# The SSD mixer of a two-block transformer kernel, with pair loop, norms and transposes re-ordered and the decay built by float32r matmuls

## The reference, cut to what matters

```python
def ssd_mixer(u, w_in, conv_w, conv_b, dt_bias, a_log, d_skip, norm_w, w_out):
    proj = u @ w_in                     # z: 2048, xbc: 3072, dt: 32
    xbc = silu(causal_dwconv(xbc, conv_w, conv_b))   # x: 2048, B: 4*128, C: 4*128
    dt = softplus(dt_raw + dt_bias);  a = -exp(a_log)
    y = ssd_chunked_scan(xs, dt, a, bm, cm) + d_skip[:, None] * xs
    y = gated_group_rmsnorm(y, z, norm_w)            # y * silu(z), norm over 512 channels
    return y @ w_out

# ssd_chunked_scan: 4 chunks of 128 positions, 32 heads of 64 channels, 4 groups of 8 heads
cs = cumsum(dt * a)                                   # within a chunk, per head
decay_in = exp(where(tri, cs[l] - cs[s], -inf))
y_diag = ((C @ B.T) * decay_in) @ (x * dt)
states = B.T @ (x * dt * exp(cs[-1] - cs))            # per chunk
entering = sum over earlier chunks of states * decay between chunks
y_off = (C @ entering) * exp(cs)
```

## Time and profile before

| | |
|---|---|
| median of three runs (3233.7 to 3242.68) | 3242.62 us |
| the profiled execution: its own time | 3239.93 us |
| its span | 3237.8 us |
| mean granted TensorE clock | 0.948 |
| busy: PE, PEld | 3023.4 us (93%), 2446.9 us (76%) |
| busy: DVE, ACT, POOL | 1459.0, 1178.9, 1307.8 us |
| the SSD mixer | from the start to 556 us |

### The profile page before, as it was taken

One profiled execution on the slowest core, in us unless ns is written; L12 is line 12 of the kernel. 1 busy time (PEld: TensorE's weight loads), 2 busy tenths in 40 slices (PEclk: granted clock), 3 DMA queues, 4 the chain that ended last, 5 costly groups with the idle time before them and its releaser, 6 DMA issues.

```text
span 3237.8 us, 33761 instructions
## 1 busy us (share of the span) xinstructions
PE 3023.4 (93%) x13476; PEld 2446.9 (76%) x13476; DVE 1459.0 (45%) x2111; ACT 1178.9 (36%) x1640; POOL 1307.8 (40%) x670
## 2 busy tenths in 40 slices
PE   6989979999999878999999998899999989999998
PEld 4866647888888766788888877797888867778886
DVE  5557761651352377354155056663422345433132
ACT  4422233542343455543244253003423334343232
POOL 4411105544444436544444546103444443054443
PEclk8989989999999989999999998579999999999999
DMA  2211103222223222233333322002323221022322
GB/s 111 95 37 40 39 14 104 92 97 94 96 97 98 72 69 67 90 98 98 98 98 98 97 79 72 1 1 65 105 93 103 86 85 64 14 91 91 104 93 83
DMA packets 74172, 253.11 MB, mean 78 GB/s; under 512 B 8353, under 2 KB 8353, under 8 KB 74017
## 3 DMA queue, kind: packets, MB, share of 16 engines
q1 hardware_dynamic: 73008, 247.55, 23.8%
q10 hardware_dynamic: 1008, 3.41, 0.3%
HBM read 248.83 MB, written 2.10 MB: 77 GB/s over the span
## 4 chain that ended last, share of the span: by engine, by line
PE 84%; DVE 8%; ACT 3%; issue 2%; DMA 1%; POOL 1%; DVEq 0%; POOLq 0%; ACTq 0%; SPq 0%
PE bank L366 22%; PE bank L368 22%; PE bank L367 22%; PE bank L1495 3%; PE bank L388 2%; PE bank L389 1%; PE bank L390 1%; PE bank L440 1%; PE bank L843 1%; PE bank L845 1%; PE bank L844 1%; DVE inv L446 1%; PE bank L856 1%; DVE lth L1340 1%; POOL wlo L2189 1%
## 5 line engine op out<-in xcount | busy, mean ns | idle before, releaser
L2189 POOL TENSOR_TENSOR wlo<-raw,whi 128x1024 fp32r<-128x1024 f32 (+2 forms) x497 | 1135.8, 2288 | 1842.4 <-ACT whi L311 1842.4
L311 ACT ACTIVATE whi<-raw 128x1024 fp32r<-128x1024 f32 (+2 forms) x497 | 501.3, 1009 | 1139.6 <-DMA raw<-in_f_up 487.2
L366 PE MATMUL bank<-h_hi,whi 128*128 128x512 f32 x2240 | 878.8, 392 | 24.5 <-ACT xbc L925 17.2
L367 PE MATMUL bank<-h_lo,whi 128*128 128x512 f32 x2240 | 873.7, 390 | 0.0
L368 PE MATMUL bank<-h_hi,wlo 128*128 128x512 f32 x2240 | 873.4, 390 | 0.0
L366 PEld LDWEIGHTS bank<-h_hi,whi 128*128 128x128 f32 x2240 | 422.3, 189 | 116.6 <-ACT xbc L925 17.7
L367 PEld LDWEIGHTS bank<-h_lo,whi 128*128 128x128 f32 x2240 | 422.1, 188 | 89.9 <-issue 2.2
L368 PEld LDWEIGHTS bank<-h_hi,wlo 128*128 128x128 f32 x2240 | 422.0, 188 | 87.8
L366 PE MATMUL bank<-act_hi,whi 128*128 128x512 f32 x864 | 336.2, 389 | 0.9 <-POOL wlo L2189 0.9
L368 PE MATMUL bank<-act_hi,wlo 128*128 128x512 f32 x864 | 336.1, 389 | 0.0
L367 PE MATMUL bank<-act_lo,whi 128*128 128x512 f32 x864 | 336.1, 389 | 0.0
(11 more groups left out here) (418 smaller groups left out, 3886.0 us busy)
## 6 DMA issues: line engine op xcount, KB each, us to landing
raw<-in_f_up SPq DMA_DIRECT2D x216, 512.0 KB, 3.5
raw<-in_f_dn SPq DMA_DIRECT2D x64, 512.0 KB, 3.4
raw<-in_ssd_xbc SPq DMA_DIRECT2D x24, 512.0 KB, 3.5
raw<-in_f_dn SPq DMA_DIRECT2D x32, 384.0 KB, 3.0
raw<-in_lru_in SPq DMA_DIRECT2D x20, 512.0 KB, 3.5
raw<-in_ev_in SPq DMA_DIRECT2D x20, 512.0 KB, 3.5
raw<-in_f_dn SPq DMA_DIRECT2D x32, 320.0 KB, 2.9
raw<-in_ssd_z SPq DMA_DIRECT2D x16, 512.0 KB, 3.5
```

Of the source, the lines that this page charges most:

```text
L311: act.activation(whi[:, s, 0:WIDTH[u]], raw[:, s, 0:WIDTH[u]], ACT.Copy).then_inc(hi_done, 1)
L366: pe.matmul(out, wh, hi, start=kt == 0, stop=False)
L367: pe.matmul(out, wh, lo, start=False, stop=False)
L2189: pool.tensor_tensor(wlo[:, s, 0:n], raw[:, s, 0:n], whi[:, s, 0:n].bitcast(F32), ALU.subtract)\
```

## The change

The mixer's work is re-ordered and partly moved:

- The dt chain moves to xbc tile 8 on VectorE and ScalarE. It now covers 128 partitions, and ends with csT cut into three fp32r parts (`cs3`, rows 0 to 31, 32 to 63 and 64 to 95). The small transposes follow tile 13, and x's transposes follow tiles 15 to 22, two sets each; VectorE takes two sets behind each tile from 16 on.
- The decay of a head is built in its bank by six fp32r matmuls: `sel3` spreads the row over the partitions, `ident_r` with `mask_r` adds -2^100 above the diagonal, and four matmuls of 128 columns, one for each chunk, take the head's own sum off. ScalarE's exp is then taken in the bank without a bias, and VectorE multiplies by C.B from there. One more fp32r matmul with `selp` gives the rows for both heads of a pair, and one exp serves both (`ec`). GpSimd builds `selp` (`pair_rows`).
- The entering part of y is a product of its own in bank 2 for both heads, scaled by `ec` afterwards.
- The group norms move into the loop, one group behind: squares summed by GpSimd and TensorE, the inverse by Ln and Exp, the low half on GpSimd, which also makes `xdd` (`decayed`).
- z uses banks 0 and 1, the output product banks 4, 5, 0 and 1. Eight z blocks go with each pair.

```diff
+        ident_r = at("ident_r", place["ident_r"], [P, P], F32R)
+        sel3 = at("sel3", place["sel3"], [P, 64], F32R)
+        selp = at("selp", BIG + 87 * KB, [P, 2, P], F32R)
...
+            def x_natural(i):
                 st.freed(pe, i)
                 if i == 0:
-                    pe.wait_ge(nat_ok, 1)
-                    pe.wait_ge(et_ok, 1)
+                    pe.wait_ge(dt_dve, 7)
+                    pe.wait_ge(dt_act, 9)
                 w(pe, xdt_ok, i - 1)
                 for c in range(NC):
                     last = pe.transpose(bank[4 + i % 2][:, c * P:(c + 1) * P], xbc[:, i, c * P:(c + 1) * P], ident[:])
                 last.then_inc(tr_x, 1)
...
+            def decay_rows(i):
+                if i == 0:
+                    pe.wait_ge(xdt_ok, NX)
+                w(pe, p_S, 2 * i)
+                for e in range(2):
+                    h = 2 * i + e
+                    pe.matmul(bank[4 + e][:], sel3[0:96, h:h + 1].broadcast_to((96, P)), cs3[0:96, :], start=True, stop=False)
+                    pe.matmul(bank[4 + e][:].rearrange("p (c l) -> p c l", c=NC), ident_r[:],
+                              mask_r[:].unsqueeze(1).broadcast_to((P, NC, P)), start=False, stop=False)
+                    for c in range(NC):
+                        last = pe.matmul(chunk(bank[4 + e], c), chunk(cs3[0:96, :], c),
+                                         sel3[0:96, 32 + h:33 + h].broadcast_to((96, P)), start=False, stop=c == NC - 1)
+                    last.then_inc(p_cs, 1)
+                g, q = (i - 1) // 4, (i - 1) % 4
+                w(pe, p_ec, i)
+                if i == 0:
+                    pe.wait_ge(g_ent, 2)
+                elif q == 1:
+                    w(pe, gn_inv, g)
+                elif q == 2 and g + 1 < SSD_G:
+                    pe.wait_ge(g_bn, g + 2)
+                elif q == 3:
+                    pe.wait_ge(g_ent, 3 * g + 5)
+                pe.wait_ge(p_sel, i + 1)
+                pe.matmul(bank[6][:], selp[0:96, i % 2, :], cs3[0:96, :], start=True, stop=True).then_inc(p_c2, 1)
+            def y_entering(i):
+                g, q = i // 4, i % 4
+                pe.wait_ge(g_ent, 3 * g + 3)
+                pe.wait_ge(p_xd, i + 1)
+                for c in range(1, NC):
+                    last = pe.matmul(chunk(bank[2], c), ent[:, c - 1, q * P:q * P + P], chunk(xbc[:, 20 + g, :], c),
+                                     start=True, stop=True)
+                last.then_inc(p_off, 1)
+            def y_diagonal(i):
+                g, q = i // 4, i % 4
+                w(pe, p_ev, i)
+                for e in range(2):
+                    pe.wait_ge(p_S, 2 * i + e + 1)
+                    for c in range(NC):
+                        last = pe.matmul(bank[3][64 * e:64 * e + 64, c * P:(c + 1) * P],
+                                         xdt[:, g, c, q * P + 64 * e:q * P + 64 * e + 64], chunk(t1[:, e, :], c),
+                                         start=True, stop=True)
+                last.then_inc(p_y, 1)
...
+            def squares(g, ec_read):
+                pe.wait_ge(gn_acc, 2 * g + 2)
+                pe.wait_ge(p_ec, ec_read)
+                pe.matmul(bank[6][:], ones[:], nacc[:], start=True, stop=False)
+                pe.wait_ge(gn_sq, 4 * g + 4)
+                pe.matmul(bank[6][:], ones[:], sqg[:], start=False, stop=True).then_inc(gn_mm, 1)
+            for t in range(2, 24):
+                st.pe_tile(pe, t, rhs_h)
+                if t == 13:
+                    natural()
+                if 15 <= t <= 22:
+                    x_natural(2 * t - 30)
+                    x_natural(2 * t - 29)
+            c_b(0)
+            b_natural(0, 0)
+            z_blocks(2)
+            states(0, 0)
+            states(0, 1)
+            z_blocks(2)
+            decay_rows(0)
+            states(0, 2)
+            z_blocks(4)
+            for i in range(NX):
+                g, q = i // 4, i % 4
+                y_entering(i)
+                if q == 1 and g:
+                    squares(g - 1, i + 1)
+                if q == 2 and g + 1 < SSD_G:
+                    b_natural(g + 1, i + 1)
+                if q == 3 and g + 1 < SSD_G:
+                    states(g + 1, 0)
+                    states(g + 1, 1, i + 1)
+                z_blocks(4)
+                y_diagonal(i)
+                if i + 1 < NX:
+                    decay_rows(i + 1)
+                if q == 2 and g + 1 < SSD_G:
+                    c_b(g + 1)
+                if q == 3 and g + 1 < SSD_G:
+                    states(g + 1, 2)
+                z_blocks(4)
...
+                act.wait_ge(dt_dve, 3)
+                act.activation(dd[:, 1, :], dd[:, 1, :], ACT.Exp).then_inc(dt_act, 1)
+                act.activation(cs3[:], csT[:], ACT.Copy).then_inc(dt_act, 1)
+                act.wait_ge(dt_dve, 5)
+                act.activation(cs_mid[:], dd[:, 0, :], ACT.Copy).then_inc(dt_act, 1)
+                act.activation(cs3[32:64, :], dd[32:64, 0, :], ACT.Copy)
+                act.wait_ge(dt_dve, 6)
+                act.activation(cs3[64:96, :], dd[64:96, 2, :], ACT.Copy).then_inc(dt_act, 1)
...
+                if t == 8:
+                    dt_chain()
+                if t == 16:
+                    act.wait_ge(tr_dt, 2)
+                    act.activation(etot[:].rearrange("p a b -> p (a b)"), bank[5][:, 0:P], ACT.Exp).then_inc(dt_act, 1)
...
+            def exps(i):
+                act.wait_ge(p_c2, i + 1)
+                w(act, p_om, i)
+                act.activation(ec[:], bank[6][:], ACT.Exp).then_inc(p_ec, 1)
+                for e in range(2):
+                    h = 2 * i + e
+                    act.wait_ge(p_cs, h + 1)
+                    act.activation(bank[4 + e][:], bank[4 + e][:], ACT.Exp).then_inc(p_E, 1)
...
+            def inverse(g):
+                act.wait_ge(gn_mm, g + 1)
+                act.activation(bank[6][:], bank[6][:], ACT.Ln, bias=eps[:], scale=1.0 / 512).then_inc(gn_ln, 1)
+                act.wait_ge(gn_ln, g + 1)
+                act.wait_ge(g_ent, 3 * min(g + 2, SSD_G))
+                act.activation(bank[7][:], bank[6][:], ACT.Exp, scale=-0.5).then_inc(gn_inv, 1)
...
+            keep_b(0)
+            keep_cb(0)
+            exps(0)
+            for i in range(NX):
+                g, q = i // 4, i % 4
+                if i:
+                    z_tanh_of(i - 1)
+                if q == 1 and g:
+                    inverse(g - 1)
+                if q == 2 and g + 1 < SSD_G:
+                    keep_b(g + 1)
+                if q >= 2 and g:
+                    for k in (2 * q - 4, 2 * q - 3):
+                        high(4 * g - 4 + k)
+                if i + 1 < NX:
+                    exps(i + 1)
+                if q == 2 and g + 1 < SSD_G:
+                    keep_cb(g + 1)
+                if i:
+                    square(i - 1)
+            z_tanh_of(NX - 1)
+            square(NX - 1)
+            inverse(SSD_G - 1)
+            for k in range(4):
+                high(12 + k)
...
+                if 16 <= t:
+                    x_natural(2 * t - 32)
+                    x_natural(2 * t - 31)
...
+            def gate(i):
+                b = zt.bank(i)[:]
+                zt.tile_ready(dve, i)
+                dve.tensor_tensor(b, b, ipre[:], ALU.mult).then_inc(z_scaled, 1)
+                dve.wait_ge(z_tanh, i + 1)
+                dve.scalar_tensor_tensor(out=b, in0=zr[:], scalar=1.0, in1=b, op0=ALU.add, op1=ALU.mult).then_inc(z_gate, 1)
+                dve.wait_ge(z_gate, i + 1)
+                dve.wait_ge(p_ev, i + 1)
+                dve.scalar_tensor_tensor(out=xbc[:, i, :], in0=xbc[:, i, :], scalar=0.5, in1=b, op0=ALU.mult,
+                                         op1=ALU.mult).then_inc(zt.free(i), 1)
+                zt.freed(dve, i)
+                dve.engine_nop().then_inc(p_g, 1)
+            def y_sum(i):
+                dve.wait_ge(p_y, i + 1)
+                dve.tensor_tensor(xbc[:, i, :], bank[3][:], xbc[:, i, :], ALU.add).then_inc(p_ev, 1)
+            def normed(j):
+                dve.wait_ge(gn_inv, j // 4 + 1)
+                dve.scalar_tensor_tensor(out=xbc[:, j, :], in0=xbc[:, j, :], scalar=col("ssd_norm", j), in1=bank[7][:],
+                                         op0=ALU.mult, op1=ALU.mult).then_inc(gn_n, 1)
+            st.freed(dve, 22)
+            dve.memset(bank[2][:, 0:P], 0.0).then_inc(p_xd, 1)
+            entering(0)
+            y = bank[2][:, P:T]
+            for i in range(NX):
+                g, q = i // 4, i % 4
+                dve.wait_ge(p_off, i + 1)
+                dve.wait_ge(p_ec, i + 1)
+                dve.tensor_tensor(y, y, ec[:, P:T], ALU.mult).then_inc(p_om, 1)
+                dve.wait_ge(p_om, i + 1)
+                dve.scalar_tensor_tensor(out=xbc[:, i, :], in0=xbc[:, i, :], scalar=col("ssd_d", i), in1=bank[2][:],
+                                         op0=ALU.mult, op1=ALU.add).then_inc(p_xd, 1)
+                if i:
```

(98 more changed lines are left out.)

333 lines of the change are left out of this document (136 added, 197 removed).

## The result

The changed kernel takes 3307.16 us (median of 4, 3304.72 to 3309.6) against 3238.16 us (median of 4, 3233.41 to 3242.68) for the kernel before: ratio 1.0213, 95% interval [1.019, 1.0236]. It is slower by 69 us; I had forecast 11.4 us more, 3254, with a range to 3280. The profiled execution took 3304.78 us, with a span of 3302.9, 65.1 above the span before.

A forecast was written before the change was run, and what follows sets the result against it. TensorE, busy 93%, was taken as the bound. Convolution stage +43.6, loop +10.1 and norms -42.3 gave +11.4 us: 3239.9 to 3251.3 profiled, 3254 as median; own range 3240 to 3268, 8 in 10 from 3218 to 3280.

The forecast's parts named there:

- Conv stage: Convolution tiles up to C.B of group 0: C.B starts at 243.1 instead of 199.5, +43.6 us.
- xdt stops: Convolution tiles 16 to 22: TensorE stands 4.65 us behind each for VectorE's xdt, seven times.
- restart cost: Convolution tiles after a stop: the next tile's first matmuls run at the low clock, losing 1.5 us.
- Start of the loop: Mixer's pair loop, from C.B to t1 of pair 0 complete: 20.8 us with a cold restart.
- One pair: Mixer's pair loop: period 12.45 us; C.B to the last pair 231.8 against 221.7 us, +10.1.
- The relay: Pair loop: VectorE, ScalarE, GpSimd in turn delay selp; seventh matmul waits until A+5.15, A being t1 complete.
- signs of being wrong: Stated failure tests: short xdt waits, selp never releasing TensorE, or decay matmuls passing 5 us after t1.
- Rival (b): Pair loop: TensorE doesn't wait for GpSimd's rows; pair falls to 9.9, about 39 us less, 3215; chance 0.10.
- The clock: Pair loop: 8 us allowed for TensorE's clock falling; 0 if it never falls, 28 at worst.
- rival (c): Pair loop runs cold: 20 us more, 3277; chance 0.14 together with tiles that stay cold.
- The narrow matmul: Decay's 128-column fp32r matmuls: start spacing bounded by 0.09 and 0.225 us; the choice said not to matter.
- Norms: Last pair to end of first two output tiles: 26.5 us instead of 68.8, -42.3, with norms inside the loop.

The follow-up runs named there:

- e_xfix: Changed kernel with VectorE taking the transposed x sets one tile earlier and etot computed ahead of tile 15; 3253.36 us.
- e_gate: Changed kernel with VectorE's sum and gate of a pair right behind that pair's t1, and its tanh at the head of ScalarE's round; 3258.85 us.
- e_order: Changed kernel with x sets taken a tile earlier, sum and gate right behind t1, and the three holders of bank 6 brought forward; 3167.47 us.
- e_rows: Changed kernel with only GpSimd's order changed: pair_rows for the next pair ahead of the split of z's low parts; 3307.34 us.
- e_bias: Changed kernel without the four 128-column matmuls per head; ScalarE's exp takes the head's column as bias, chunk by chunk; 3290.51 us.

## Why the prediction was wrong

**Conv stage, +43.6.** Right: +41.0. The order of the code gave the xdt stops before the trace could (4.65 forecast from a row of the kernel before, seven times 4.65 measured). The restart cost is right too: behind the set at 190.80 the tile's first eight matmuls take 3.55 us (192.39 to 195.94) where eight warm ones take 1.8, so 1.7 lost where I took 1.5. e_xfix takes that whole term away: the delay was the order of two loops, not work. By the rule that I weighed there (the Trainium skill, "TensorE: Matmul & The Clock Gate", Part 4: transposes don't bring full clock) a tile would have lost up to 2.9. The rows lie nearer to my value, but they can't say what the transposes did for the rise: it came at 195.9, after 3.5 us of fp32r matmuls.

**Start of the loop, 20.8.** Right: t1 of pair 0 was complete 20.7 us after `C.B`.

**One pair, +10.1 for the loop. This is the step that failed**, and it carries the error: from `C.B` to the end of the last pair 293.2 us, not 231.8, so +71.5 and not +10.1. The step says that the seventh matmul waits for `selp` and that "four z blocks 2.74" lie behind it to cover VectorE's 3.2. I priced those z blocks and never asked what they wait for. The two z banks are named in the change; with them the first z block of a tile can't start before `gate(i-1)`, and that is behind t1(i). So VectorE's chain isn't covered by z: it is followed by scaling, tanh and gate (309.15 to 311.9; TensorE stands 4.2 us there, in the fourteen stops 5.1 on average), then by the z blocks, the first eight of their twelve matmuls at 1.2 GHz (0.43 a start in place of 0.23), and only then by `y_diagonal`. t1 to t1 took 270.1 us in the fifteen intervals (18.0 each) against 210.1 with the clock's 8. The miss in these intervals is 60 us. e_gate shows the cause of most of it: with the gate (and the sum and tanh that it needs) moved ahead, the wait is gone and 49 us of the loop with it, though new stops of 31.4 us came at L917. With those away too (e_order) the loop is 82 us shorter than in the kernel after, and shorter than I had forecast. What the cut to two z banks has in it by itself is read from the code; no run gives z a third bank.

**The relay.** Its time was right: `selp` was complete at 314.55, 5.3 us behind t1, where I had put the seventh matmul at A+5.15. What was wrong is that TensorE waits for it: it comes to L917 only at 319.88, 10.7 behind t1, and e_rows gives nothing. Two of my signs of being wrong thus came true: `selp` never releases TensorE, and the decay matmuls pass A+5. Rival (b) had that, but expected a faster kernel from it: a wait that doesn't bind gives nothing back when another is longer. **The clock.** I put down 8 us. In the shares above, 25 us lie between the loop with and without its stops. So rival (c)'s effect was there, but with the stops at the z blocks and not with a stop at the decay. **The narrow matmul.** My lower bound was right (0.10 us), but "it doesn't matter" was not: as the relay doesn't bind, it lies on TensorE's path, 17 us in e_bias.

**Norms, -42.3.** Right: from the last `y_diagonal` (533.7) to the end of the first output tiles (557.65) 24.0 us. The same mark in the kernel before lies at 489.55, not at my rounded 490, so the stage took 68.4 there and the change is -44.4. The rows in the kernel after:

```profile
540.43 1.28 ACT L1069 ACT_TABLE_LOAD   x1
...
545.58 1.02 PE L947 MATMUL bank<-sqg,ones 128*128 128x512 f32 x2
546.64 0.66 ACT L1069 ACTIVATE bank<-bank,eps 128x512 f32<-128x512 f32 x1 [4.93 <-PE bank L947]
547.32 1.28 ACT L1072 ACT_TABLE_LOAD   x1
548.62 0.58 ACT L1072 ACTIVATE bank<-bank 128x512 f32<-128x512 f32 x1
...
550.72 5.03 POOL L2381 TENSOR_TENSOR g_lo<-xbc,g_hi 128x512 fp32r<-128x512 f32 x4 [8.68 <-ACT g_hi L1076]
551.71 0.39 PE L398 MATMUL bank<-g_hi,wlo 128*128 128x512 f32 x1
552.08 0.50 PE L396 MATMUL bank<-g_hi,whi 128*128 128x512 f32 x1
```

Ln and Exp still take a load each, as in the earlier trace rows. The first lies in time in which ScalarE waits for the squares. The second delays the first low half (four in 5.03 us, so at about 551.98), but TensorE has matmuls until then: from the start at 551.71 to the next at 552.08 there are 0.37 us where 0.23 is the pace. So the second load costs TensorE some 0.1 us here. The Trainium skill ("ScalarE: Activation LUTs", table sets) has both functions in one set; this compiled kernel didn't go by that.

The sum: 41.0 + 71.5 - 44.4 = 68.1, and the span grew by 65.1; the 3.0 us between them lie behind the first output tiles, and the executions of the kernel before alone differ by 9.3. Not tried: a third bank for z. Nor was the 12.7 us stop at tile 11 taken away; it stands, at 12.5 to 12.7, in the kernel after and in all eight variants.

## What to carry to other kernels

Work that is meant to cover a wait has waits of its own. Before such a filler (here the z blocks) is counted as cover, ask which buffer it writes, who frees that buffer, and where that operation stands in its engine's queue: here it stood behind the very chain that the filler was to cover. When a change cuts the number of buffers, look for its price (here it wasn't measured by itself), and when a stage has two suspected waits, work out both, since removing the shorter one gives nothing. And where an engine runs in order, try moving the operation that frees a buffer ahead before moving the arithmetic from engine to engine: order was worth 140 us here (3307 to 3167), the choice between bias and matmul 17 at most.

## What the runs showed of the hardware

A stop of 4 to 6 us cost TensorE more than its length: 37.9 us less of standing in the convolution stage brought `C.B` 58.3 us forward in e_xfix, and the loop's instructions took 199.0 us of busy time at a granted clock of 0.84 and 173.8 at 0.95. In e_gate the L917 matmul behind a stop of 3.79 to 4.91 us has a record of 0.76 to 0.77 us, and behind a stop of 1.53 us one of 0.47, as without a stop (0.45). Four fp32r matmuls of 128 columns over 96 rows take 0.40 us from start to start (318.57 to 318.97), where one of 512 columns takes 0.23: for the same 512 columns the narrow form costs 1.7 times as much.
